# A transformer chain of two blocks on one core: ScalarE's exponential ahead of the copy of turned values, compressed keys' products beside the projections, the RG-LRU's clamp and the borders' root on ScalarE

## The reference

```python
for layer in range(2):                                 # first block
    h = rms_norm(x, norm_mix_pre[layer])
    h = dilated_attention(h) if layer == 0 else rglru(h)
    x = x + rms_norm(h, norm_mix_post[layer])
    h = conv_ffn(rms_norm(x, norm_ffn_pre[layer]))     # gelu(g) * v, hidden width 3072
    x = x + rms_norm(h, norm_ffn_post[layer])
# rglru: r, i = sigmoid gates of the convolved xb; log_a = 8 r log_sigmoid(lam)
#   a = exp(log_a); b = sqrt(max(-expm1(2 log_a), 0)) * i * xb
#   hs[t] = a[t] * hs[t-1] + b[t]; out = (hs * gelu(gb)) @ w_out

for l in range(2):                                     # second block
    z = _rmsnorm(x, norm_g[l]) @ w_in[l]               # queries, keys, values, gates
    # _nsa: compressed keys and values: windows of 32 tokens, stride 16 (31 of them),
    #   silu((window + pe) @ w1) @ w2 with w1 2048x128; compressed, selected and
    #   sliding-window attention, mixed by sigmoid gates
    # _fox: causal attention with a cumulative forget bias
    # _memory_xattn: attention on _rmsnorm(mem) @ w_mem_kv, 256 memory rows
    u = g0 * (o_a @ w_branch_a) + g1 * (o_b @ w_branch_b) + g2 * (o_m @ w_branch_m)
    x = x + u @ w_out[l]
```

## Time and profile before

| | before |
|---|---|
| time, median of 3 runs (lowest to highest) | 3017.97 us (3016.29 to 3022.12) |
| profiled execution: time, span | 3021.99 us, 3020.5 us |
| TensorE busy, mean granted clock | 2976.1 us (99%), 0.997 |
| GpSimd busy | 1939.0 us (64%) |
| VectorE busy | 1497.1 us (50%) |
| ScalarE busy | 807.1 us (27%) |
| moved to and from memory | 87 GB/s on average |

### The profile page before, as it was taken

The page is one execution under the profiler, slowest core; times in us unless marked ns, Lnnn a source line. Parts: engine busy times, 40 slices in busy tenths (PEclk is TensorE's granted clock), DMA queues, the critical chain, the costliest instruction groups (busy, mean ns, idle before and its releaser), DMA issues.

```text
span 3020.5 us, 41671 instructions
## 1 busy us (share of the span) xinstructions
PE 2976.1 (99%) x15422; PEld 2495.9 (83%) x15422; DVE 1497.1 (50%) x3021; ACT 807.1 (27%) x1755; POOL 1939.0 (64%) x2192
## 2 busy tenths in 40 slices
PE   9999999999999999999999999999999999999999
PEld 7888887888888878888888887788888988888887
DVE  3333334477730684777213746663334654664332
ACT  1111111322210452222112225552112213564110
POOL 6555554599987788999775862125777684112775
PEclk9999999999999999999999999999999999999999
DMA  4222232122332222323323221011224332011232
GB/s 168 93 90 89 93 105 67 57 98 98 98 98 98 72 82 77 98 98 98 111 91 126 94 95 43 29 36 64 98 98 140 100 103 70 29 43 36 91 98 91
DMA packets 70216, 261.47 MB, mean 87 GB/s; under 512 B 8320, under 2 KB 8832, under 8 KB 68224
## 3 DMA queue, kind: packets, MB, share of 16 engines
q1 hardware_dynamic: 65696, 232.81, 23.6%
q10 hardware_dynamic: 4320, 25.99, 2.4%
HBM read 251.43 MB, written 2.10 MB: 84 GB/s over the span
## 4 chain that ended last, share of the span: by engine, by line
PE 88%; POOL 5%; DVE 3%; issue 2%; ACT 2%; DMA 0%; ACTq 0%; DVEq 0%; SPq 0%; POOLq 0%
PE bank L400 23%; PE bank L402 23%; PE bank L401 23%; POOL w_lo L2314 3%; PE bank L1959 3%; PE bank L1944 1%; PE bank L708 1%; POOL w_hi L2310 1%; PE bank L427 1%; PE bank L440 1%; PE bank L432 1%; PE bank L1660 1%; PE bank L428 1%; PE bank L680 1%; PE bank L1366 1%
## 5 line engine op out<-in xcount | busy, mean ns | idle before, releaser
L2314 POOL TENSOR_TENSOR w_lo<-w_raw,w_hi 128x256 fp32r<-128x256 f32 x1728 | 1406.7, 844 | 36.1
L2310 POOL TENSOR_SCALAR w_hi<-w_raw 128x1024 fp32r<-128x1024 f32 x432 | 489.9, 1134 | 1014.6 <-PE bank L402 918.7
L400 PE MATMUL bank<-in_hi,w_hi 128*128 128x512 f32 x1408 | 554.8, 394 | 0.7 <-POOL w_lo L2314 0.7
L402 PE MATMUL bank<-in_hi,w_lo 128*128 128x512 f32 x1408 | 548.6, 390 | 0.0
L401 PE MATMUL bank<-in_lo,w_hi 128*128 128x512 f32 x1408 | 547.8, 389 | 0.0
L400 PE MATMUL bank<-z_hi,w_hi 128*128 128x512 f32 x976 | 392.4, 402 | 0.4 <-POOL w_lo L2314 0.4
L402 PE MATMUL bank<-z_hi,w_lo 128*128 128x512 f32 x976 | 381.2, 391 | 0.0
L401 PE MATMUL bank<-z_lo,w_hi 128*128 128x512 f32 x976 | 380.7, 390 | 0.0
L402 PEld LDWEIGHTS bank<-in_hi,w_lo 128*128 128x128 f32 x1408 | 264.3, 188 | 56.0
L400 PEld LDWEIGHTS bank<-in_hi,w_hi 128*128 128x128 f32 x1408 | 264.5, 188 | 53.0 <-issue 1.1
L401 PEld LDWEIGHTS bank<-in_lo,w_hi 128*128 128x128 f32 x1408 | 264.7, 188 | 52.8
(11 more groups left out here) (441 smaller groups left out, 5161.5 us busy)
## 6 DMA issues: line engine op xcount, KB each, us to landing
w_raw<-in_units SPq DMA_DIRECT2D x434, 512.0 KB, 3.4
bias<-in_bias ACTq DMA_DIRECT2D x8, 1152.0 KB, 5.1
o_all<-in_cmp_w ACTq DMA_DIRECT2D x4, 2048.0 KB, 8.5
x_res<-in_x ACTq DMA_DIRECT2D x4, 512.0 KB, 7.6
mem_in<-in_mem ACTq DMA_DIRECT2D x2, 1024.0 KB, 8.6
nsa_q_hi<-nsa_q_hi SPq DMA_DIRECT2D x16, 128.0 KB, 2.5
nsa_q_lo<-nsa_q_lo SPq DMA_DIRECT2D x16, 128.0 KB, 2.3
out<-x_res ACTq DMA_DIRECT2D x4, 512.0 KB, 2.6
```

What stands on the lines that cost most here:

```text
L400: pe.matmul(out, hi[:, w], rh, start=start and n == 0, stop=False)
L402: last = pe.matmul(out, lo[:, w], rh, start=False, stop=stop and n == len(tiles) - 1)
L2310: d = c.s.unit_hi.on(pool.tensor_scalar(c.w_hi[s][:, :], c.w_raw[s][:, :], 1.0, 0.0, ALU.mult, ALU.add))
L2314: last = pool.tensor_tensor(c.w_lo[s][:, w], c.w_raw[s][:, w], c.w_hi[s][:, w].bitcast(F32), ALU.subtract)
```

## The change

- `act_attend`: in each step the exponential of task `now` is issued ahead of the copy of task `now - 2`.
- `pe_compress` no longer runs in one go. `pe_unit` calls `beside(n)` behind each tile; in steps 5 and 6 (keys) and 9 and 10 (values), behind the last four tiles of the first unit and the first four of the second, it issues four of the 32 products. The generator's other steps keep their places on TensorE; on ScalarE both compressed steps come one step later, and with the keys' one the load of the second `w1`.
- RG-LRU: the clamp leaves VectorE; ScalarE does it as `Relu(-x)` ahead of its square root. VectorE scans groups 0 to 3 ahead of the roots of 6 and 7; ScalarE takes one output ahead of each gelu.
- Borders: VectorE writes mean + eps, ScalarE takes its square root, VectorE forms the reciprocal and one Newton step. `act_out` issues a small square root ahead of its last bank. The fillers between the two sums go, of the ten behind them seven stay. VectorE splits chunk 0 ahead of scaling chunk 1, and is one chunk less behind from there on.

```diff
--- before.py
+++ after.py
@@ -389,7 +389,7 @@
 
-def pe_unit(pe, c, key, jobs):
+def pe_unit(pe, c, key, jobs, beside=lambda n: None):
 
@@ -400,6 +400,7 @@
             last = pe.matmul(out, lo[:, w], rh, start=False, stop=stop and n == len(tiles) - 1)
+            beside(n)
     pe_unit_done(c, key, last)
@@ -409,8 +410,8 @@
 
-def pe_project(pe, c, key, out, hi, lo, k0=0, start=True, stop=True):
-    pe_unit(pe, c, key, [(out, [(k, hi[:, k0 + k, :], lo[:, k0 + k, :]) for k in range(DC)], start, stop)])
+def pe_project(pe, c, key, out, hi, lo, k0=0, start=True, stop=True, beside=lambda n: None):
+    pe_unit(pe, c, key, [(out, [(k, hi[:, k0 + k, :], lo[:, k0 + k, :]) for k in range(DC)], start, stop)], beside)
 
@@ -491,10 +492,9 @@
     pe_add_tokens(pe, c, c.bank[sums], c.acc, True)
-    pe_warm(pe, c, b, 3)
     pe.wait_ge(*c.s.squared[name, DC - 1])
     c.s.tokens_summed.on(pe_add_tokens(pe, c, c.bank[sums], c.sq[(DC - 1) % 2], False), ("post", name))
-    pe_warm(pe, c, b, 10)
+    pe_warm(pe, c, b, 7)
     pe.wait_ge(*c.s.bank_copied[name, DC - 1])
@@ -579,10 +579,24 @@
 
+def post_work(c, name):
+    return bank_columns(c.bank[POST_BANKS[name == "attn_out"][1]], WORK, TT)
+
+
 def dve_post_begin(dve, c, name, gain):
+
     dve.wait_ge(*c.s.tokens_summed["post", name])
-    b = c.bank[POST_BANKS[name == "attn_out"][1]]
-    c.s.factor_found.on(dve_rsqrt(dve, c, c.narrow[:, 0:TT], b[:, 0:TT], bank_columns(b, WORK, TT), 1.0 / D), ("post", name))
+    mean, a = post_work(c, name)
+    r, step = c.narrow[:, 0:TT], c.s.dve_step
+    step.on(dve.tensor_scalar(mean, c.bank[POST_BANKS[name == "attn_out"][1]][:, 0:TT], 1.0 / D, EPS, ALU.mult, ALU.add), ("mean", name))
+    dve.wait_ge(*c.s.act_step["mean_root", name])
+    d = step.on(dve.reciprocal(r, a))
+    dve.wait_ge(*d)
+    d = step.on(dve.tensor_tensor(a, mean, r, ALU.mult))
+    dve.wait_ge(*d)
+    d = step.on(dve.scalar_tensor_tensor(a, a, -0.5, r, ALU.mult, ALU.mult))
+    dve.wait_ge(*d)
+    c.s.factor_found.on(dve.scalar_tensor_tensor(r, a, 1.5, r, ALU.add, ALU.mult), ("post", name))
     dve.wait_ge(*c.s.factor_spread["post", name])
@@ -623,9 +637,11 @@
     for k in range(DC + 1):
+        if k == 1:
+            dve_norm_chunk(dve, c, z, 0)
         if post and k < DC:
             dve_post_chunk(dve, c, post, gain, k)
-        if k >= 1:
+        if k >= 2:
             dve_norm_chunk(dve, c, z, k - 1)
@@ -652,6 +668,11 @@
         c.s.bank_copied.on(act.activation(c.y[:, n, :], b[:, :], ACT.Copy), (name, n))
+        if n == DC - 2:
+            act.activation(c.narrow[:, TT:TT + 1], c.ones[:, 0:1], ACT.Sqrt)
+    mean, root = post_work(c, name)
+    act.wait_ge(*c.s.dve_step["mean", name])
+    c.s.act_step.on(act.activation(root, mean, ACT.Sqrt), ("mean_root", name))
 
@@ -1101,7 +1122,9 @@
 def act_lru_sqrt(act, c, ch):
-    act.wait_ge(*c.s.dve_step["root", ch])
+    act.wait_ge(*c.s.dve_step["open", ch])
+    d = c.s.act_step.on(act.activation(c.th[:, ch, :], c.th[:, ch, :], ACT.Relu, scale=-1.0))
+    act.wait_ge(*d)
     c.s.act_step.on(act.activation(c.th[:, ch, :], c.th[:, ch, :], ACT.Sqrt), ("sqrt", ch))
@@ -1144,8 +1167,8 @@
     for ch in range(5, DC):
+        act_lru_out(act, c, 2 * ch - 9)
         act_lru_gelu(act, c, ch)
-        act_lru_out(act, c, 2 * ch - 9)
         act_lru_out(act, c, 2 * ch - 8)
@@ -1177,9 +1200,7 @@
     dve.wait_ge(*c.s.act_step["decay", ch])
-    d = step.on(dve.scalar_tensor_tensor(c.th[:, ch, :], c.lru_t[ch % 2][:, :], 1.0, c.th[:, ch, :], ALU.add, ALU.mult), ("open", ch))
-    dve.wait_ge(*d)
-    step.on(dve.tensor_scalar(c.th[:, ch, :], c.th[:, ch, :], -1.0, 0.0, ALU.mult, ALU.max), ("root", ch))
+    step.on(dve.scalar_tensor_tensor(c.th[:, ch, :], c.lru_t[ch % 2][:, :], 1.0, c.th[:, ch, :], ALU.add, ALU.mult), ("open", ch))
 
@@ -1220,13 +1241,13 @@
     dve_lru_gb(dve, c, z, 0)
-    dve_lru_scan(dve, c, 0)
-    dve_lru_scan(dve, c, 1)
+    for ch in range(4):
+        dve_lru_scan(dve, c, ch)
     dve_lru_root(dve, c, 6)
     for ch in range(DC):
-        if ch >= 2:
+        if ch >= 4:
             dve_lru_scan(dve, c, ch)
@@ -1298,6 +1319,7 @@
 SLOTS_TWO = 35
+COMPRESS = (5, 9)
 
@@ -1335,6 +1357,14 @@
     compressed, memory = pe_compressed(pe, c, layer), pe_memory(pe, c, zm)
+    products = [pe_compress(pe, c, layer, which) for which in range(2)]
+
+    def pe_beside(m):
+
+        def beside(n):
+            if m in COMPRESS and n >= DC // 2 or m - 1 in COMPRESS and n < DC // 2:
+                next(products[COMPRESS.index(m if m in COMPRESS else m - 1)])
+        return beside
     c.free = {b: None for b in range(8)}
@@ -1346,7 +1376,7 @@
                 hi, lo = (zm.hi, zm.lo) if s.memory else (z.hi, z.lo)
-                pe_project(pe, c, ("z", layer, m), c.bank[m % 4][:, 0:s.n], hi, lo)
+                pe_project(pe, c, ("z", layer, m), c.bank[m % 4][:, 0:s.n], hi, lo, beside=pe_beside(m))
             c.free[m % 4] = c.s.squared["ep", layer, m] if s.kind in ("q", "k") else c.s.evicted["z", layer, m]
@@ -1651,20 +1681,22 @@
 def pe_compress(pe, c, layer, which):
-    yield
     b = c.bank[5]
         m = pe.matmul(b[:, 0:2 * NC], c.w1[:, l * P:l * P + P], c.xw[:, l, :], start=l == 0, stop=l == CMP_L - 1)
-    c.s.compressed.on(m, (layer, which))
-    yield
+        if l == CMP_L - 1:
+            c.s.compressed.on(m, (layer, which))
+        if l % 4 == 3:
+            yield
 
     cb, w2 = c.bank[5], c.cols[:, layer, C_W2:C_W2 + P + HD]
-    yield from pe_compress(pe, c, layer, 0)
+    yield
+    yield
     pe.wait_ge(*c.s.dve_step["cmp", layer, 0])
@@ -1678,7 +1710,8 @@
     c.free[6] = c.s.stored["cmp", layer]
-    yield from pe_compress(pe, c, layer, 1)
+    yield
+    yield
     yield
@@ -1964,12 +1997,6 @@
     for now in range(STEPS):
-        if 0 <= now - 2 < TASKS:
-            t = tasks[now - 2]
-            act.wait_ge(*c.s.turned[t.t])
-            if t.index >= 3:
-                act.wait_ge(*c.s.weighted[t.t - 3])
-            c.s.turned_out.on(act.activation(c.at_pt[t.index % 3][:, 0:t.keys], c.bank[3 + t.index % 2][:, 0:t.keys], ACT.Copy), t.t)
         if now < TASKS:
@@ -1983,6 +2010,12 @@
             c.s.exponentials.on(m, t.t)
+        if 0 <= now - 2 < TASKS:
+            t = tasks[now - 2]
+            act.wait_ge(*c.s.turned[t.t])
+            if t.index >= 3:
+                act.wait_ge(*c.s.weighted[t.t - 3])
+            c.s.turned_out.on(act.activation(c.at_pt[t.index % 3][:, 0:t.keys], c.bank[3 + t.index % 2][:, 0:t.keys], ACT.Copy), t.t)
         n, step = divmod(now, CHUNK)
             act.wait_ge(*c.s.logits_ready[tasks[now - 1].t])
```

## The result

The changed kernel takes 3085.66 us (median of 4 runs, 3076.07 to 3089.34) against 3020.05 us for the kernel before (4 runs): ratio 1.0213, 95% interval 1.0199 to 1.0227. It is slower by 64 us by that ratio. The prediction was 3032 us, range 3018 to 3042: right in sign, too small by 54 us.

What follows compares the result with a forecast made beforehand. TensorE, busy 2976.1 of 3020.5 us, was taken to bound the kernel. 3021.99 - 6.5 (clock) + 20.2 (waits) + 3.4 (clock) - 9.2 (borders) - 0.5 (RG-LRU) + 2.5 (attention) = 3031.9, say 3032 us; range 3018 to 3042.

Steps and rivals of the forecast that it cites:

- the clock, -6.5 + 3.4: Compressed products: spreading them saves 6.5 us of low clock in layer 0; low clock after the (c) waits costs 3.4.
- Rival 4: The clock falls in the product stretches too, now with idle time among them: 3035 to 3042 us, chance 0.14.
- (c): Step 9: without the block as cover, TensorE waits 6.0 us a layer for VectorE's chain before spreading the memory factor.
- (a): Keys' products, unit 5: the first burst waits 2.4 us a layer for VectorE's window sums.
- (b): Values' products, unit 9: the first burst waits 1.7 us a layer for VectorE's window sums.
- Rival 1: The moved products hide, with no new waits (a) to (c): 3008.3 us, faster; chance 0.08.
- the borders, -9.2: Four borders: root on ScalarE, fewer fillers and VectorE's earlier first split save 2.3 us each (-5.6 to -10.4 in all).
- -0.5 for the wait ahead of L432: Borders: VectorE splitting the first chunk earlier mostly removes TensorE's 0.63 us wait, 0.5 us saved a border.
- RG-LRU, -0.5: Recurrence: clamps leave VectorE, but it stays busy and GpSimd disturbed, so only 0.5 us is saved.
- Rival 2: Recurrence: TensorE's wait for GpSimd goes, as the port rule has it: 6 us less, 3026; chance 0.11.
- attention, +2.5: Exponential ahead of the copy: losses slightly exceed gains, +0.2 to +0.4 us a pass, +2.5 over 8 passes.
- Rival 3: Attention: the exponential's new order pays and rows come sooner, -6 instead of +2.5: 3023.4 us; chance 0.12.

Runs made afterwards that it cites:

- inputs_ready: As spread_later, but the products multiply columns of their own weights and don't wait for the window sums: 3038.98 us, ratio 1.0069 to the kernel before.
- spread_later: Kernel before with only the products beside the projections, and the memory factor's spread moved behind the seventh tile of unit 10: 3069.91 us, ratio 1.0170.
- data_control: inputs_ready with the waits for the window sums put back; differs from spread_later only in the numbers multiplied: 3070.74 us, ratio 1.0172 to the kernel before.
- clamp: Kernel before with only the RG-LRU part, the clamp on ScalarE and the new orders there: 3019.70 us, ratio 1.0003.
- exp_first: Kernel before with only ScalarE's exponential ahead of the copy in the second block's attention: 3032.34 us, ratio 1.0043.
- borders_old_order: Kernel before with the borders' root on ScalarE, but VectorE's old order of scaling and splitting chunks: 3015.23 us, ratio 0.9980.
- borders: Kernel before with only the borders' part of the change, VectorE's new chunk order included: 3012.86 us, ratio 0.9982.
- products: Kernel before with only the compressed keys' products moved beside the projections: 3077.21 us, ratio 1.0186.
- early_block: As spread_later, but all 32 products in one go behind the fifth tile of units 5 and 9: 3067.17 us, ratio 1.0152 to the kernel before.
- thin: As inputs_ready, but bursts of two products behind each of sixteen tiles instead of four behind eight: 3029.77 us, ratio 1.0030 to the kernel before.

## Why the prediction was right and wrong

**Failed: the clock, -6.5 + 3.4, read from the profiles +40.** The step was "Spread in eight bursts of 8 instructions between full tiles the products cost the same, 8 x 0.9 = 7.2 us a block, and the small matmuls are diluted. I credit -6.5." The small matmuls were not diluted: the bursts lowered the clock by themselves (inputs_ready, 15 us at half), and with the new waits just ahead of them for twice as long (spread_later, data_control, 28 us). Why they do stays open. Rival 4 named the low clock in the product stretches, with idle time among them, but priced a stretch at 6.5 us, the one low stretch that the trace of before held; those of the changed kernel cost 12 to 15 each, which put the time outside the range. And the estimate for (c) took its length from the wait in the recurrence, a wait followed by dense products. Such a wait did get such a stretch where it stayed alone (3.02 us and then 4 us at 0.57 in inputs_ready); the new waits of the changed kernel have bursts behind them. A price should have been sought for both at once, and none was in the trace: its absence was the reason for a wider upper end.

The credit itself was rightly read: of 21 runs of the kernel before in the first comparison 13 took 3015.3 to 3018.3 us (mean clock 0.998 or 0.999) and 8 took 3021.5 to 3023.8 us (0.996 or 0.997). Over the four comparisons of the experiments it is 34 of 70 runs above 3021 us. That the old block is what they lose can be seen in three more kernels that keep it. In the traces of clamp (3023.04 us) and exp_first the block of layer 0's values takes 11.33 and 11.42 us for 7.34, and in that of borders_old_order (3015.76 us, mean clock 0.997) 15 us at 0.56 stand at the keys of layer 1; in that of borders (3012.56 us, 0.998) no block is hit. So there were 6 us to win in about half of the runs, and the change paid 40 for them.

**Held: (a), (b), (c).** 2.4, 1.7 and 6.0 us a layer were forecast, 2.13, 1.45 and 6.00 are layer 0's rows; 20.2 forecast and 19.2 measured in all. (Of (c), the prediction's "16 products that used to stand there" are 32, 16 for each of the two units.) VectorE's chain behind the sums (first and last row of 28):

```profile
1683.93 0.22 DVE L1611 SCALAR_TENSOR_TENSOR bank<-bank,z_factor_square 128x48 f32<-128x48 f32 x1 [10.41 <-PE bank L1396]
...
1689.68 0.16 DVE L554 SCALAR_TENSOR_TENSOR mem_factor_by_token<-bank,mem_factor_by_token 128x2 f32<-128x2 f32 x1
```

5.9 us, as in the earlier trace rows, now with no products over it. Rival 1 (the products hide) is out.

**Off in size: the borders, -9.2, measured -5.4 (-8.1 to -2.7).** TensorE, then ScalarE and VectorE at the border of the earlier trace rows:

```profile
984.48 1.05 PE L506 MATMUL bank<-ones,square 128*128 128x1 f32 x8
...
991.77 0.73 PE L433 MATMUL bank<-in_lo,w_hi 128*128 128x512 f32 x2 [0.62 <-DVE in_lo L529]
...
993.15 0.48 PE L428 MATMUL bank<-in_hi,w_hi 128*128 128x512 f32 x1
...
995.71 0.49 PE L428 MATMUL bank<-in_hi,w_hi 128*128 128x512 f32 x1
...
998.00 0.48 PE L428 MATMUL bank<-in_hi,w_hi 128*128 128x512 f32 x1
```
```profile
985.57 0.17 DVE L591 TENSOR_SCALAR bank<-bank 128x4 f32<-128x4 f32 x1 [16.35 <-PE bank L506]
985.96 0.18 DVE L593 RECIPROCAL narrow<-bank 128x4 f32<-128x4 f32 x1 [0.22 <-ACT bank L675]
...
986.59 0.16 DVE L599 SCALAR_TENSOR_TENSOR narrow<-bank,narrow 128x4 f32<-128x4 f32 x1
```

The chain is 985.57 to 986.75, 1.2 us instead of 2.4 (1.3 was forecast). From the end of the first sums to the first `lo` product it is 991.77 - 984.48 = 7.3 us, before 994.90 - 985.86 = 9.0: 1.8 sooner, the 1.1 + 0.7 of the prediction. The failed half-step is the last one, -0.5 for the wait ahead of L432: it is still 0.62. The split of chunk 0 does start sooner, but waits for ScalarE's `hi` and then takes 1.72 us (1.35 before in the same place), here VectorE in the run with the borders alone:

```profile
582.74 1.72 DVE L528 SCALAR_TENSOR_TENSOR in_lo<-x_res,gains,in_hi 128x512 fp32r<-128x512 f32 x1 [0.19 <-ACT in_hi L513]
```

And the third chunk's products start 2.56 us behind the second's (993.15 to 995.71), the fourth's 2.29 behind those: 0.3 lost. The cause is in the order: only chunk 0's split moved ahead, so VectorE now scales chunks 2 and 3 between the first two splits. From the split of chunk 1 on the order is the old one; VectorE is not one chunk less behind there. So 1.5 us a border by the timelines. Two slips of the prediction's working changed little: 0.17 us is a 128 x 4 step of VectorE, not a 128 x 1 one, and the smallest gain comes to -6.0 by its own terms, not -5.6.

**Not to be told from nothing: RG-LRU, -0.5 (bounds 0 and -6.5), measured +0.9 (-1.8 to +3.6).** GpSimd's quarter splits in 1062 to 1117, changed kernel:

```profile
L2347 POOL TENSOR_TENSOR w_lo<-w_raw,w_hi 128x256 fp32r<-128x256 f32 x35 | 41.0, 1200 | 0.7
```

1200 ns against 1160 in the earlier trace rows, and the wait for it 5.3 instead of 4.8 us. In the run with this part alone VectorE is still busy for 53.64 of these 55 us (53.28 before). Rival 2 is out. The low stretch behind the wait is longer too (5.35 us of work at 0.59 against 4.72 at 0.66), but not by this part: the mean clock from 1100 to 1150 us is 0.93 in the traces of products, spread_later, data_control and early_block as well, which have the old clamp, and 0.97 in that of before. The Trainium skill's lock of the port pair (SBUF - State Buffer, SBUF: two separate sides) is neither shown nor refuted by that: VectorE was full of work either way. Only its strict reading, 5.7 us won, did not come true. ScalarE around the new operation:

```profile
1067.95 1.28 ACT L1128 ACT_TABLE_LOAD   x1
1069.25 0.63 ACT L1128 ACTIVATE tanh_sqrt_h<-tanh_sqrt_h 128x512 f32<-128x512 f32 x1
1069.78 0.61 ACT L1126 ACTIVATE tanh_sqrt_h<-tanh_sqrt_h 128x512 f32<-128x512 f32 x1
1070.43 0.63 ACT L1128 ACTIVATE tanh_sqrt_h<-tanh_sqrt_h 128x512 f32<-128x512 f32 x1
```

L1126 is the Relu, L1128 the root: one load ahead of the first root and none between them. The Trainium skill (ScalarE: Activation LUTs, Table sets) says that relu is in every set; these rows agree for the root's set.

**Mis-sized: attention, +2.5 (bounds -6 and +10), measured +13.0 (+9 to +17).** The mechanism is the forecast one, the exponential waiting for a late maximum with the copy behind it. ScalarE, then TensorE, of exp_first:

```profile
1885.19 0.78 ACT L1977 ACTIVATE at_p<-bank,at_st,nsa_scale 128x512 f32<-128x512 f32 x1 [0.67 <-DVE at_st L2068]
...
1885.95 0.27 ACT L1985 ACTIVATE at_pt<-bank 128x128 f32<-128x128 f32 x1
...
1886.27 0.49 PE L1959 MATMUL bank<-cmp_v,at_pt 128*128 128x128 f32 x2 [0.57 <-ACT at_pt L1985]
```

ScalarE idles 0.67 us for the maximum; the copy stands behind it and the exponential, and TensorE pays 0.57 for it. In that kernel the weighted values wait 14.3 us in 34 places for the copy, and 9.0 us in 14 places for which the profile names no releaser, against 16.5 us for rows before, of which 7.5 are left. The term was sized by following ten tasks of one pass, where losses and gains nearly cancelled. Over all passes they don't: 23.3 us of new waits against 9.0 fewer for rows and 3.5 for probabilities, 10.4 net by the views of waits (0.4 for copies was there before). That is already at the upper bound. Rival 3 (the exponential pays) is out.

## What to carry to other kernels

A block of small products in one place may be covering waits elsewhere: before cutting it up, list what becomes ready under it. Where TensorE is at 99%, first ask of an edit what it does to the granted clock, and if the trace has neither the idle time nor the mix of products that the edit makes, the upper end is open. On an engine that works in order, the operation whose input comes last belongs behind the one whose input is there.

## What the runs showed of the hardware

- Products of 62 columns set between dense ones, 0.9 us at a time with no idle time at all, brought the granted clock to 1.2 GHz for 14 or 15 us at two places of four (inputs_ready). With a wait of 1.4 or 2.1 us ahead of them it was 28 to 31 us, again not at every place. With the same waits ahead of dense products and the small ones in one block later, the traced run kept full clock and six of ten runs did not. In the three kinds of kernel the clock cost some 15, 38 and 4 us over before.
- A wait of 3.02 us ahead of dense products was followed by 4 us at 0.57 (inputs_ready), one of 2.63 us by a low clock till 2401 us, some 6 us (thin).
- The places hit differ between kernels with the same products and waits (layer 0's keys in after, layer 1's in products), and the runs of products spread over 21 us, with mean clocks from 0.979 to 0.987.
- ScalarE's root of 128 x 4: VectorE idles 0.22 us for it, hand-over both ways included (0.3 was forecast).
